# Token-major up-projection: one transpose per column group, its partition quadrants placed by DMA through memory

## What is computed

```python
def conv_ffn(h, w_up, conv_w, conv_b, w_down):
    u = jnp.einsum('bsd,df->bsf', h, w_up)
    S = u.shape[1]
    y = conv_b
    for tap in range(CONV_WIDTH):
        shifted = jnp.pad(u, ((0, 0), (tap, 0), (0, 0)))[:, :S]
        y = y + shifted * conv_w[CONV_WIDTH - 1 - tap]
    val, gate = jnp.split(y, 2, axis=-1)
    return jnp.einsum('bsf,fd->bsd', jax.nn.silu(gate) * val, w_down)
```

## Time and profile before

| | |
|---|---|
| median of three runs | 1942.24 us |
| profiled execution, whole | 1942.34 us |
| profiled execution, span from first to last instruction | 1940.2 us |
| granted TensorE clock, mean | 0.998 |
| TensorE busy | 1924.7 us, 99% |
| VectorE busy | 1428.8 us, 74% |
| ScalarE busy | 1111.5 us, 57% |
| DMA engines, mean busy share of q1 | 56.2% |

### The profile page before, as it was taken

How to read it: one execution, slowest core, us unless ns; L and a number is a source line. 1 busy time by engine, 2 the same in 40 slices (tenths; PEclk the granted TensorE clock), 3 DMA queues, 4 the chain that set the end, 5 groups by cost and what they waited for, 6 DMA issues and landing times.

```text
span 1940.2 us, 30192 instructions
## 1 busy us (share of the span) xinstructions
PE 1924.7 (99%) x10550; PEld 1665.1 (86%) x10550; DVE 1428.8 (74%) x2242; ACT 1111.5 (57%) x1845; POOL 48.7 (3%) x53
## 2 busy tenths in 40 slices
PE   8999999999999999999999999999999999999998
PEld 8888888888888888888888888888888888888887
DVE  6667786767877777777666667877777777756665
ACT  6555544656565656666544556656665566655544
POOL 0002250000000000000000000000000000000000
PEclk9999999999999999999999999999999999999999
DMA  9655555555555555555555555555555555555653
GB/s 327 196 172 160 183 164 169 190 184 190 195 183 187 193 192 182 188 194 168 200 203 191 193 173 177 192 193 183 188 194 191 182 189 195 190 170 191 214 191 108
DMA packets 205203, 364.93 MB, mean 188 GB/s; under 512 B 6563, under 2 KB 49100, under 8 KB 205132
## 3 DMA queue, kind: packets, MB, share of 16 engines
q1 hardware_dynamic: 203388, 362.34, 56.2%
q10 hardware_dynamic: 1744, 1.63, 0.3%
HBM read 361.83 MB, written 2.11 MB: 188 GB/s over the span
## 4 chain that ended last, share of the span: by engine, by line
PE 98%; DVE 1%; ACT 0%; DMA 0%; issue 0%; DVEq 0%; SPq 0%
PE ps L391 41%; PE ps L395 20%; PE ps L498 8%; PE ps L500 8%; PE ps L501 8%; PE ps L464 7%; PE ps L468 3%; PE ps L482 0%; PE ps L484 0%; PE ps L485 0%; DVE ssq L1245 0%; DVE lo L1115 0%; PE ps L670 0%; PE ps L672 0%; PE ps L530 0%; PE ps L583 0%
## 5 line engine op out<-in xcount | busy, mean ns | idle before, releaser
L741 ACT ACTIVATE hi<-raw 128x512 fp32r<-128x512 f32 x1352 | 844.4, 630 | 792.7 <-PE ps L395 470.0
L1115 DVE TENSOR_TENSOR lo<-raw,hi 128x512 fp32r<-128x512 f32 x1360 | 927.9, 697 | 465.1 <-ACT hi L741 459.1
L391 PE MATMUL ps<-h,hi 128*128 128x512 f32 x2816 | 958.2, 394 | 0.0
L395 PE MATMUL ps<-h,lo 128*128 128x256 f32 x2816 | 734.3, 277 | 0.0
L391 PEld LDWEIGHTS ps<-h,hi 128*128 128x128 f32 x2816 | 508.2, 188 | 98.1 <-DVE lo L1115 0.2
L395 PEld LDWEIGHTS ps<-h,lo 128*128 128x128 f32 x2816 | 529.2, 188 | 25.4
L498 PE MATMUL ps<-hi,act 128*128 128x512 f32 x528 | 205.6, 389 | 0.0
L500 PE MATMUL ps<-lo,act 128*128 128x512 f32 x528 | 205.6, 389 | 0.0
L501 PE MATMUL ps<-hi,act 128*128 128x512 f32 x528 | 205.5, 389 | 0.0
L464 PE MATMUL ps<-h,hi 128*128 128x512 f32 x576 | 183.3, 400 | 0.0
L468 PEld LDWEIGHTS ps<-h,lo 128*128 128x128 f32 x576 | 108.3, 188 | 25.4
(11 more groups left out here) (191 smaller groups left out, 1493.8 us busy)
## 6 DMA issues: line engine op xcount, KB each, us to landing
raw<-in_w_up SPq DMA_DIRECT2D x176, 1024.0 KB, 5.0
raw<-in_w_down SPq DMA_DIRECT2D x88, 1024.0 KB, 5.0
raw<-in_w_in SPq DMA_DIRECT2D x54, 1024.0 KB, 5.1
raw<-in_w_out SPq DMA_DIRECT2D x16, 1024.0 KB, 5.1
raw<-in_pool_w SPq DMA_DIRECT2D x4, 1024.0 KB, 5.2
raw<-in_w_in SPq DMA_DIRECT2D x8, 256.0 KB, 4.9
x<-in_xT SPq DMA_DIRECT2D x8, 128.0 KB, 4.7
x<-in_xT SPq DMA_DIRECT2D x2, 512.0 KB, 7.8
```

The costliest lines, as they stand in the source:

```text
L391: pe.matmul(ps[:, bank + m, :], hi[:, kt, m * P:(m + 1) * P], mv, start=first and kt == 0, stop=False, skip_group_check=True)
L395: return pe.matmul(ps[:, bank + m, S:2 * S], lo[:, kt, m * P:(m + 1) * P], mv[:, 0:S], start=False, stop=last and kt == KT - 1, skip_group ...
L741: a_.activation(hi[:, kt, :], raw[:, slot, kt, :], ACT.Copy).then_inc(hi_done, 1)
L1115: ve.tensor_tensor(lo[:, kt, :], raw[:, slot, kt, :], hi[:, kt, :].bitcast(F32), ALU.subtract).then_inc(lo_done, 1)
```

## The change

The first group of each layer stays wide. The other 42 groups become token units. Their result has tokens on partitions and has to be turned to feature-major:

- `turn_up` (VectorE) does one transpose instruction of 128 partitions x 1024 elements from PSUM to `turned_u` (the memory of `sqt`). It transposes blocks of 32x32, so each block is right inside and stands in the wrong quadrant of partitions.
- `rows_away` (ScalarE's queue) stores the 512 KB to `bounce` in device memory, once `evacuated` says that the transpose is done.
- `quads_back` (ScalarE's queue) waits until the store has landed (`rows_out`) and issues four loads of 128 KB, one for each quadrant of 32 partitions, into `quads_u` (the memory of `sqacc`).
- `scale_turned` (VectorE) waits for the four loads and multiplies by the norm, in two instructions of 128 x 512, into `u`.

`first_half`, `up_add` and `up_scale` go for these groups. The taps move later: `tap0` to window 0 of the next group, `conv0` and `tap1` to window 3; `silu` and `gate_values` go from window 3 of the value group to window 1 of the gate group.

```diff
-            def token_unit(n, acc, first, last, j, ready=None, src=h):
+            def token_unit(n, acc, first, last, j, ready=None, src=h, base=0):
...
-                            wide_unit(U_UP[l] + 4 * gt + j, i * (8 * KT), wide_bank(G), j == 0, j == UP_UNITS - 1,
-                                      lambda kt: h[:, KT * j + kt, :], split if first and gt == 0 else None,
-                                      None if first else opening(j))
+                            if first and gt == 0:
+                                wide_unit(U_UP[l] + j, 0, wide_bank(G), j == 0, j == UP_UNITS - 1,
+                                          lambda kt: h[:, KT * j + kt, :], split)
+                            else:
+                                token_unit(U_UP[l] + 4 * gt + j, ps[:, wide_bank(G):wide_bank(G) + 2, :], j == 0,
+                                           j == UP_UNITS - 1, j, base=i * (8 * KT))
...
+            def rows_away(Gv):
+
+                sc_e.wait_ge(evacuated, Gv + 1)
+                sc_e.dma_start(bounce, turned_u).then_inc(rows_out, 16)
+
+            def quads_back(past):
+
+                sc_e.wait_ge(rows_out, past)
+                for q in range(4):
+                    there = quads_u[q * TURN:(q + 1) * TURN, :].rearrange("f (b e) -> f b e", b=4)
+                    here = bounce.rearrange("(b f) (q e) -> q f b e", b=4, q=4)[q]
+                    sc_e.dma_start(there, here).then_inc(quad_in[q], 16)
...
                         if j == 0:
-                            first_half(q, i * (8 * KT) + KT * U_UP[l], G_UP[l] - 1)
+                            rows_away(i * 2 + (G_UP[l] - 1))
                         if j == 1:
+                            quads_back(i * 32 + (16 * (l * (2 * PAIRS - 1)) - 16))
+                        if j == 3:
                             conv0(q, i - 1, l, 1)
-                        if j == 3:
-                            silu(q)
...
                             else:
-                                conv0(q, i, l, 0)
+                                quads_back(i * 32 + 16 * (l * (2 * PAIRS - 1)))
+                                silu(i * 2 + (l * 2 * PAIRS - 1))
+                        if j == 3 and not peel:
+                            conv0(q, i, l, 0)
...
+            def turn_up(unit_end, Gp):
+
+                ve.wait_ge(w_used, unit_end)
                 b = wide_bank(Gp)
...
+                rows = ps[:, b:b + 2, :].rearrange("p t (m q f) -> p q (t m) f", m=4, q=4)
+                ve.transpose(turned_u.rearrange("p (q k s) -> p q k s", q=4, k=8), rows).then_inc(evacuated, 1)
+
+            def scale_turned(l, past):
+
+                for q in range(4):
+                    ve.wait_ge(quad_in[q], past)
...
                         if j == 0:
-                            up_sum(q, i * 2 + G_UP[l], G_UP[l])
+                            turn_up(i * (8 * KT) + KT * (U_UP[l] + 4), G_UP[l])
+                            tap0(i * 2 + (l * 2 * PAIRS - 1), i - 1, l, 1)
                         if j == 1:
+                            gate_values(i + (l * PAIRS - 1))
+                        if j == 2:
+                            scale_turned(l, i * 32 + 16 * (l * (2 * PAIRS - 1)))
+                        if j == 3:
                             tap1(q, i, l, 0)
-                        if j == 2:
-                            tap0(q, i, l, 0)
-                        if j == 3:
                             act_lo_pair(i + (l * PAIRS - 1), i - 1)
```

More of the change, by code:

```diff
@@ L244, in trunk_kernel @@
         u_ready = sem("u_ready")
+        rows_out = sem("rows_out")
+        quad_in = [sem(f"quad_in{i}") for i in range(4)]
         y0 = sem("y0")
@@ L1035, in g_windows @@
                         if j == 0:
-                            first_half(q, i * (8 * KT) + KT * (U_UP[l] + 4), G_UP[l])
+                            if peel:
+                                first_half(l)
+                            else:
+                                rows_away(i * 2 + G_UP[l])
                             if peel and l == 1:
@@ L1055, in _ @@
                     if j == 0:
-                        first_half(q, KT * U_DN[l], G_DN[l] - 1)
+                        rows_away(G_DN[l] - 1)
                     if j == 1:
+                        quads_back(16 * ((l + 1) * (2 * PAIRS - 1)))
+                    if j == 3:
                         conv0(q, PAIRS - 1, l, 1)
-                    if j == 3:
+                    if j == 5:
                         silu(q)
-                    if j == 5:
+                    if j == 6:
                         act_hi_pair((l + 1) * PAIRS - 1, PAIRS - 1)
@@ L1381, in _, with up_add, up_scale @@
                     add_mixed(n // 4 - 1)
-            def up_add(q, Gp):
-                b = wide_bank(Gp)
[L1386 to L1397, removed]
+            def up_add(l):
+                b = wide_bank(G_UP[l])
+                ve.wait_ge(sum_a, l + 1)
+                ve.tensor_tensor(u[:, :, :], u[:, :, :], ps[:, b:b + 4, S:2 * S], ALU.add).then_inc(evacuated, 1)
+            def up_scale(l):
+                ve.wait_ge(evacuated, G_UP[l] + 1)
+                ve.tensor_tensor(u[:, :, :], u[:, :, :], rstd_4, ALU.mult).then_inc(u_ready, 1)
+            def turn_up(unit_end, Gp):
+                ve.wait_ge(w_used, unit_end)
+                b = wide_bank(Gp)
+                rows = ps[:, b:b + 2, :].rearrange("p t (m q f) -> p q (t m) f", m=4, q=4)
[3 more added lines that the diff above has]
+                    ve.wait_ge(quad_in[q], past)
+                for t in range(2):
+                    quads = quads_u.rearrange("p (b t m s) -> p t m b s", b=4, t=2, m=4)[:, t]
+                    out = u[:, :, t * P:(t + 1) * P].rearrange("p m (b s) -> p m b s", b=4)
+                    r = rstd[:, t * P:(t + 1) * P].rearrange("p (b s) -> p b s", b=4).unsqueeze(1).to_broadcast([P, 4, 4, TURN])
+                    scaled = ve.tensor_tensor(out, quads, r, ALU.mult)
+                scaled.then_inc(u_ready, 1)
             def tap1(q, i, l, gt, ms=range(4)):
@@ L1491, in v_windows @@
                         if j == 0:
-                            up_sum(q, i * 2 + (G_UP[l] - 1), G_UP[l] - 1)
-                        if j == 1:
+                            turn_up(i * (8 * KT) + KT * U_UP[l], G_UP[l] - 1)
+                            tap0(i * 2 + (l * 2 * PAIRS - 2), i - 1, l, 0)
+                        if j == 2:
+                            scale_turned(l, i * 32 + (16 * (l * (2 * PAIRS - 1)) - 16))
+                        if j == 3:
                             tap1(q, i - 1, l, 1)
-                        if j == 2:
-                            tap0(q, i - 1, l, 1)
-                        if j == 3:
-                            gate_values(i + (l * PAIRS - 1))
                 def g_first():
@@ L1502, in g_first @@
                     w_lo(U_UP[l] + 4, 0, 0)
-                    up_add(q, G_UP[l])
+                    up_add(l)
                     if l == 1:
@@ L1509, in g_first @@
                     ve.wait_ge(rstd_ready, 2 * l + 2)
-                    up_scale(G_UP[l])
+                    up_scale(l)
                     def taps(kt):
@@ L1541, in _ @@
                     if j == 0:
-                        up_sum(q, G_DN[l] - 1, G_DN[l] - 1)
-                    if j == 1:
+                        turn_up(KT * U_DN[l], G_DN[l] - 1)
+                        tap0(q - 1, PAIRS - 1, l, 0)
+                    if j == 2:
+                        scale_turned(l, 16 * ((l + 1) * (2 * PAIRS - 1)))
+                    if j == 3:
                         tap1(q, PAIRS - 1, l, 1)
-                    if j == 2:
+                    if j == 4:
                         tap0(q, PAIRS - 1, l, 1)
-                    if j == 3:
+                    if j == 5:
                         gate_values((l + 1) * PAIRS - 1)
-                    if j == 6:
+                    if j == 7:
                         act_lo_pair((l + 1) * PAIRS - 1, PAIRS - 1)
```

18 lines of the change are left out of this document (10 added, 8 removed).

## The result

| | before | after |
|---|---|---|
| median | 1942.3 us (1942.01 to 1942.56) | 2042.64 us (2035.62 to 2045.8) |
| profiled execution | 1942.34 us | 2042.72 us |
| its span | 1940.2 us | 2040.6 us |
| mean granted clock | 0.998 | 0.987 |

The ratio after to before is 1.0511 (95% interval 1.0498 to 1.0523). The direction was forecast, the size was not: 2004.6 with a range to 2025. The prediction expected a net loss of 62 us. The net loss is 100.

The account below looks back on a forecast made before the run. TensorE, busy 99% of the span, was taken to bound the kernel. From 1942.3 us, 18.5 came off for faster matmuls and 80.8 was added for waits before unit 2: 2004.6 us, range 1960 to 2025.

Parts of the forecast that it names:

- The gain: TensorE's matmuls in 42 groups: 672 kt change form, each 0.0275 us faster, 18.5 us in all.
- Window 0: VectorE's transpose takes 1.27 us, ScalarE issues the store at 2.82, and unit 1 is not late: no loss.
- The store: ScalarE's 512 KB store waits for the weight DMA issued before it, whatever its queue, and lands at 8.2 us.
- transfers share: Rival, chance 0.10: packets of both queues alternate, the store lands before 7.16, S = 8.9, total 1943 us, no change.
- The issue held: Window 1, ScalarE: a weight DMA holds the first load's issue until 9.12; four loads issued, ScalarE free at 10.66.
- issue not held: Rival, chance 0.22: first load issued at 8.25, S = 10.2, waits of 2.28 and 0.72 us, total 1985 us.
- S: Time after a group's start on TensorE when ScalarE is free of the four load issues in window 1: 10.66 us.
- The waits before unit 2: TensorE waits for ScalarE's late hi: 2.74 us in 20 gate groups, 1.18 in 22 other groups, 80.8 us in all.
- What stays hidden: Loads land at 13.7, scale_turned needs to start by 15.4 for unit 3, later weights cost nothing: no loss.
- slower still: Rival, chance 0.11: long transpose (+12.6 us) or loads landing after 15.4 (22 us per us): 2017 us and more.
- The clock: TensorE's clock was read at its upper level, 2.4 GHz shown as 1.00, in both stretches; no loss was priced.

Follow-up runs that it names:

- the kernel without the trip: Kernel after the change with store and loads left out, scale_turned reading the turned rows in place (output not the reference's): 1925.08 us, ratio 0.991.
- experiment 5: Kernel after the change, but SP issues window 0's weight DMA only once the store has landed: 1965.19 us, ratio 1.0122.
- the short-wait kernel: Kernel without store and loads, plus three extra ScalarE instructions ahead of silu in each of 20 gate groups: 1955.49 us, ratio 1.007.
- the 4 KB pieces: Kernel after the change, its four loads taking whole 4 KB rows instead of 1 KB pieces (output not the reference's): 2038.43 us, ratio 1.0502.
- the long-wait kernel: Kernel without store and loads, plus five extra ScalarE instructions ahead of silu in each of 20 gate groups: 2043.12 us, ratio 1.0515.

## Why the prediction was right in kind and short in size

**The gain** was right: 17.4 of 18.5 us, from the kernel without the trip (1925.1 us, where the sum had 1923.8), with `hi` to `hi` at 842.29 - 840.93 = 1.36 us. The wide form had eight matmuls in 1.3875 us where the token form has six in 1.36, for the same columns: by this estimate each of the two that went cost 14 ns beside its columns.

**Window 0** was right. The transpose was put at 1.27 us, and all 42 take 1.24 (L1429: min/median/max in ns), the store was put at 2.82 after the group's start and comes at 2.75, and unit 1 is never late:

```profile
L1429 DVE STREAM_TRANSPOSE sqt<-ps x42: 1239/1243/1246, 484.0 to 1784.8; 128x1024 f32<-128x1024 f32 x42
```

**The store** behind the weights was right, landing put at 5.4 us after its issue and 5.9 in the trace (the store's line, L949, over all 42):

```profile
DMA to landing us min/median/max: 2.6/5.9/6.3
```

The rival *transfers share* is refuted for the store behind the weights, which is where it was set up. Its witness is the DMA view from 830.4 to 833.8, just after the store's issue:

```profile
q1 hardware_dynamic: 453, 0.92, 90.5%
q10 hardware_dynamic: 7, 0.03, 2.0%
```

SP's queue q1 moved 453 packets, ScalarE's q10 seven. From 834.2 to 835.6 it is the other way round:

```profile
q10 hardware_dynamic: 110, 0.39, 67.4%
q1 hardware_dynamic: 7, 0.01, 2.4%
raw<-in_w_up SPq DMA_DIRECT2D x1, 1024.0 KB, 7.4
```

The last line is unit 1's weight DMA, issued at 834.47, with its time to landing.

The rule of the Trainium skill weighed there (DMA: Bandwidth & Descriptors, section "Queues, rings and completion order") is that an engine takes turns between the rows that have work, packet by packet. The page gives 9 to 17 descriptors as typical of its packets and 64 as their limit. In the profile the 1 MB is 512 pieces of 2 KB, 32 for each of 16 engines: if these are its descriptors, turns of the typical size do not agree with the rows above, and a turn near the limit would. No run here tells which it was.

**The issue held** was wrong, and by luck its error was cancelled by another. No first load was held until 9.12 in the groups read above. The four issues took 1.76 us in a row right after the landing, and the landing was half a microsecond later than I had it. ScalarE was free at 837.83 - 827.29 = 10.54 and 861.44 - 850.81 = 10.63, against 10.66. Held issues do occur, as in the earlier trace rows, but less and not every time. The step took them for a rule. In 24 of the 42 trips the four took 1.76 to 1.78 us, in the rest up to 2.65, and the single ones (ns, min/median/max):

```profile
L957 ACTq DMA_DIRECT2D sqacc<-turned_rows x168: 309/453/1074, 491.2 to 1794.2; - x168
```

The rival *issue not held* had the mechanism of the issues and the wrong landing: it would give 1985, and ScalarE's time of 10.2 was not seen. The lower end of the range does not follow from it as stated: an S lower by 1 us than 10.2 gives 1923.8 + 20 x 1.28 = 1949, and 1960 stands for 0.6 us.

**The waits before unit 2** were right. Counted as delay against the time at which unit 2 was due, 839.24 - 838.17 = 1.07 us in the value group (1.18 forecast) and 864.41 - 861.69 = 2.72 in the gate group (2.74 forecast). Over the trace the 40 stops before unit 2 show 73.5 us of idle time, with 0.30 each 85.5, where 80.8 were forecast for 42. The sum hides four differences. The 20 value groups took 23.0 us of idle time (1.45 each with the restart, against 1.18), 5.4 us too much. The 18 gate groups took 46.5 (2.88 each, against 2.74), 2.6 too much. The two first down-projection groups took 1.99 each where 1.18 was put, 2.2 too much with the restart. And the gate groups of the two last pairs did not wait at all, since no weights stood ahead of their store, which takes 5.5 off. Issues that took longer than 1.76 us add up to 5.9 us over the 42 trips, a part of the excess.

**What stays hidden** is the first step that failed. It put the loads' landing at 13.7 after the group's start and saw no wait before unit 3. The last of them landed at 843.2, which is 15.9, past the deadline of 15.4 that the same paragraph names. The term that was mis-sized is the landing of unit 1's weights, "12.1, later by little": it came at 834.47 + 7.4 = 841.9, which is 14.6 after the start. The 1.6 us from there to the loads' landing held (1.3). The DMA view of 838.6 to 840.6 shows part of the delay:

```profile
q10 hardware_dynamic: 446, 0.41, 83.8%
q1 hardware_dynamic: 70, 0.11, 17.3%
```

From 835.9, when the store had landed, to 838.6 only q1 moved anything; then the last 70 packets of the weights moved beside the loads, and both landed late. So between weights and loads the order of issue did not hold strictly, as in experiment 5. The case *slower still* named late loads and put 22 us to each us; here 13 stops before unit 3 cost 5.8 + 13 x 0.30 = 9.7 us. Why both transfers end so late is open: loads with no weights just ahead need 2.8 us, larger pieces do not help, and no run changed their 32 partitions each.

**The clock** is the second step that failed, and the larger one. The prediction read the clock at 1.00 in the earlier trace rows, where TensorE has no gap, and kept it for a kernel with 42 gaps, without ever naming this as an assumption. What the runs showed in its place: stops of 1.9 us and more can bring the lower clock, here at 13 of 21, at 13 x 1.70 = 22.1 us in the profiled execution.

In numbers, from the forecast of 2004.6 to 2042.7: 1.3 for the gain, 85.5 - 80.8 = 4.7 for the waits before unit 2, 9.7 for those before unit 3, 22.1 for the clock, 37.8 in all of 38.1. The range ended at 2025: the clock had no share in it, and late loads only the half of the last rival.

## What to carry to other kernels

Price a wait on the engine that sets the time in two parts, its length and what follows when the engine starts again: here stops of 1.2 us cost 1.5, and stops of 3.4 us cost 5.9. Where an engine computes for the path that sets the time, keep a wait for a DMA off its queue unless the landing is sure to come in time: the same trip cost 118 us on ScalarE's queue behind the weights, 40 us there with no weights ahead of the store, and nothing on SP's queue ahead of the next weights. When a small transfer is on a tight path, look at what was issued just before and just after it, on any queue.

## What the runs showed of the hardware

- **A store waited for the weights issued before it, across queues.** 512 KB from ScalarE's queue landed in 5.9 us when SP's 1 MB had been issued 1.0 us ahead, and in 2.6 with nothing ahead. From GpSimd's queue it took 5.4 us (median) with the 1 MB 1.3 us ahead.
- **Loads into 32 partitions and weights did not keep that order.** In experiment 5 the two queues moved 0.47 and 0.92 MB in the same 5 us (852 to 857), and the loads needed 6.9 us where they need 2.8 with no weights just ahead.
- **The granted clock around a stop.** At stops of up to 1.7 us it stayed at 1.00, in all 211 of them in six kernels (32 in the kernel after, 20 of 1.23 us in the short-wait kernel). At 19 of 45 stops of 1.8 to 3.0 us (13 of 21 in the kernel after, 4 of 18 with the 4 KB pieces), and at 20 of 20 of 3.40 us, it fell to 0.50, for 3.4 us in the kernel after and for 3.4 or 6.8 us in the long-wait kernel. It fell between 0.8 us before and 1.6 us after the restart. At which of the 45 it falls is open.
- **A stop costs 0.30 us more than the idle time shown** (twenty of 1.23 us cost 30.4 us in the short-wait kernel).
- **Issuing a DMA holds the issuing engine**: 0.44 us each in a row on ScalarE's and SP's queue (four in 1.76 us, up to 2.65 in the kernel after), 0.55 on GpSimd's (four in 2.18 us).
- **A transpose of 128 x 1024 from PSUM takes 1.243 us**, not four times the 0.446 us of one of 32 x 256, so turning 512 KB in one instruction is cheap; it is the way into the right partitions that costs.
